# The first two weight chunks after a layer norm, taken one after the other instead of interleaved by K-tile

## The chip, the cores and the metric

The kernel runs on one core of a Trainium2 chip. The metric is device time in microseconds (us) for one execution of the whole program; lower is better. A core has a tensor engine (PE, with its weight loads shown as PEld), a vector engine (DVE), a scalar engine (ACT), a general engine (POOL) and a queue that starts DMAs (SP). Each runs its own instructions in order, and they meet through semaphores.

## The reference

512 tokens of 1024 features pass through a first block of two layers and then a second block of two layers. The part in which the change lies is the first block:

```python
for i in range(2):
    h = swiglu(x, ffn1_w_gate[i], ffn1_w_up[i], ffn1_w_down[i])
    x = layer_norm(ALPHA * x + 0.5 * h, ln_gain[i, 0], ln_bias[i, 0])
    m = pool_mixer(x, ...) if i == 0 else dilated_attention(x, ...)
    x = layer_norm(ALPHA * x + m, ln_gain[i, 1], ln_bias[i, 1])
    h = swiglu(x, ffn2_w_gate[i], ffn2_w_up[i], ffn2_w_down[i])
    x = layer_norm(ALPHA * x + 0.5 * h, ln_gain[i, 2], ln_bias[i, 2])
```

`swiglu(x, g, u, d)` is `(silu(x @ g) * (x @ u)) @ d` with 2816 hidden features. Everything is float32. After the first block come two layers with retention, sparse attention and gated linear attention, which the kernel calls `mixer`.

## The kernel before

Activations lie feature by feature: `x`, and its high and low parts `xh` and `xl`, are 8 K-tiles of 128 features by 512 tokens. A float32 product is made of three faster ones, `wh*xh + wh*xl + wl*xh`. POOL makes `wh` and `wl` out of the raw weights (L349, L353), chunk by chunk. A chunk is 1024 rows (8 K-tiles) by 256 columns, so two output tiles `m` of 128 features. It is split in four quarters of two K-tiles each. There are two slots for split weights, taken in turn: POOL may start on chunk c+2 only when PE has finished chunk c (it waits for `acc` at L342), and PE waits for each quarter (`wait_chunk`, L366). SP loads the raw weights ahead. One chunk for all 512 tokens is 2 x 8 x 3 = 48 matmuls of 512 columns.

The program is a list of stages: ffn 0, pool, ffn 1, ffn 2, attn, ffn 3, mixer, mixer. Between two of them lies a layer norm. It works in two halves of the tokens, h = 0 and h = 1, of 256 each. For each half DVE and ACT produce the normalized K-tiles in order: DVE scales tile m (L792), ACT writes `xh` (L719), DVE writes `xl` (L799) and raises `acts`. The tile is then ready for PE. DVE does all 8 tiles of half 0 and then all 8 of half 1. In between, after tile 5 of half 0 is scaled, DVE waits for the statistics of half 1 (L779). They come from PE: `pe_half_sums(before, 1)` (L521) issues matmuls against a matrix of ones at L534, ACT squares the result (L698) before it goes on with tile 5, and DVE goes on from there.

PE meets the new activations in `pe_first` (L546). It treats the first two chunks of the new stage, c and c+1, half by half, 6 matmuls of 256 columns for one K-tile of one chunk (L572):

- half 0: chunk c goes K-tile by K-tile as the tiles come, and chunk c+1 follows two K-tiles behind (`LAG = 2`). Ahead of the first two K-tiles stand 5 matmuls each that compute nothing (`pe_spin`, L544). After the third step stand the sums for half 1.
- half 1: chunk c first, K-tile by K-tile with a wait for each, and then chunk c+1 without any wait for activations.

Chunk c is finished, and its slot free for POOL, after chunk c of half 1. `pe_first` runs at five layer norms: before pool (border 0 in this text), ffn 1 (border 1), ffn 2 (border 2), attn (border 3, where a half is written in another order of tokens) and ffn 3 (border 4). The first ffn starts with `pe_begin`, and the borders into and between the mixers have `pe_entry` with an interleave of its own. After `pe_first` come whole chunks through `product` (L378, matmuls at L387) or `piece` (L889, matmuls at L1895), all with 512 columns.

Of the kernel before, what the change touches and what calls it, by code (L numbers as in the profile page):

```python
# [25 lines left out]
P = 128  # L26
# [3 lines left out]
KT = D // P  # L30
# [188 lines left out]
class Kernel:  # L219
# [326 lines left out]
    def pe_first(self, pe, st, residue=False):  # L546

        s, c = self.s, st.chunk0
        before = self.stages[self.stages.index(st) - 1]
        if before.kind == "start":  # L550
            self.pe_begin(pe, st)
            return
        for h in range(2):
            for step in range(2 * KT):
                for n in range(2):
                    k = step - (self.LAG, KT)[h] * n
                    if not 0 <= k < KT:
                        continue
                    if n == 0:
                        if h == 0 and k < 2:  # L560
                            self.pe_spin(self.VAR_BANK[1], 0, 5)
                        pe.wait_ge(s["acts"].sem, st.at("acts", KT * h + k + 1 - 2 * KT))
                    if (h, n, k) == (0, 1, 0):
                        pe.wait_ge(s["z_ready"].sem, st.at("z_ready", 0))
                    if h == 0 and k % 2 == 0:
                        self.wait_chunk(pe, c + n, k // 2)
                    xh, xl = (self.half(a[:, k], h, residue) for a in (self.xh, self.xl))
                    for m in range(2):
                        out = self.half(self.ps[:, 2 * n + m], h, residue)
                        w = slice(k * 256 + m * P, k * 256 + m * P + P)  # L570
                        for q, (a, b) in enumerate(((self.wh, xh), (self.wh, xl), (self.wl, xh))):
                            mm = self.nc.tensor.matmul(out, a[:, (c + n) % 2, w], b, start=k == 0 and q == 0, stop=k == KT - 1 and q == 2)  # L572
                        if h == 1 and k == KT - 1:
                            s["acc"].up(mm)
                if h == 0 and step == 2:
                    self.pe_half_sums(pe, before, 1)

    def pe_last(self, pe, st, chunks, xs, residue=False, sums=None):

        s = self.s  # L580
        xh, xl = xs
        at = 0
        sums = sums or self.pe_half_sums
        for n, (c, k, ready) in enumerate(chunks):
            last = n == len(chunks) - 1
            self.wait_chunk(pe, c)
            if ready:
                ready()
            for m, h in (((0, 0), (1, 0), (0, 1), (1, 1)) if last else ((0, 0), (0, 1), (1, 0), (1, 1))):
                if n == 0 and (m, h) == (0, 0) and "z_ready" in st.per:  # L590
                    pe.wait_ge(s["z_ready"].sem, st.at("z_ready", 4))
                out = self.tail_out(h, m, residue)
                for t in range(k):
                    if last and t == 3 and m != h:
                        sums(pe, st, 0, (2,) if h else (0, 1))
                    w = slice(t * 256 + m * P, t * 256 + m * P + P)
                    for q, (a, b) in enumerate(((self.wh, xh), (self.wh, xl), (self.wl, xh))):
                        mm = self.nc.tensor.matmul(out, a[:, c % 2, w], self.half(b(at + t), h, residue),  # L598
                                                   start=n == 0 and t == 0 and q == 0, stop=last and t == k - 1 and q == 2)
                if last and h == 0:  # L600
                    s["tail_mm"].up(mm)
                if h == 1:
                    s["acc"].up(mm)
            at += k
# [2404 lines left out]
```

## Time and profile before

| | us |
|---|---|
| median of 3 runs | 3483.22 |
| lowest and highest | 3482.59, 3483.66 |
| the profiled execution | 3485.5 |
| its span, first to last instruction | 3483.7 |

The profile is of one execution. Its page gives the busy time of each engine, the chain of work that ended last, and the costliest groups of instructions. The trace behind it gives every instruction with its start from the beginning of the span, its duration, and, where the engine stood idle ahead of it, what released it. Matmuls overlap each other, so their pace is read from the distance of their starts and not from their durations. The granted clock says which share of the full speed TensorE had: 1.00 is 2.4 GHz and 0.50 is 1.2 GHz.

### The profile page before, as it was taken

To read this page: it belongs to the slowest core of one execution; us is meant where nothing else is said; L and a number is where in the kernel's file an instruction comes from. 1 tells how busy PE (TensorE), PEld (TensorE's weight loads), DVE (VectorE), ACT (ScalarE), POOL (GpSimd) and SP (SyncE) were. 2 spreads that over 40 slices of the span, in tenths; PEclk is the share of its full clock that TensorE was granted. 3 is DMA by queue.
4 is the path that set the end of the run, shared out by engine and by line. 5 is a ranking of instruction groups with operands and counts; after the bars stand their busy time and mean duration, and the time that the engine had idled before them with its cause. 6 is when DMAs were issued, how large, how long until landed. Compare 5 with 4: busy or idle time off the path is not lost.

```text
span 3483.7 us, 48672 instructions
## 1 busy us (share of the span) xinstructions
PE 3421.0 (98%) x18708; PEld 2830.2 (81%) x18708; DVE 1503.3 (43%) x2307; ACT 822.7 (24%) x1463; POOL 2521.6 (72%) x2220
## 2 busy tenths in 40 slices
PE   9999989999999999999999999999999999999998
PEld 7887978888988888888888887877778787777876
DVE  5562562112311143344456114265656436565643
ACT  1110232110211022222234111122323222232322
POOL 9998787888788877665655888856566785655675
PEclk9999999999999999999999999999999999999999
DMA  6553222322233222122211332222222222222222
GB/s 220 189 182 102 83 85 85 96 93 92 93 96 95 89 93 88 63 72 73 73 62 49 108 96 94 85 82 67 62 72 67 85 85 85 64 61 76 64 82 73
DMA packets 322475, 312.08 MB, mean 90 GB/s; under 512 B 11616, under 2 KB 306176, under 8 KB 322048
## 3 DMA queue, kind: packets, MB, share of 16 engines
q1 hardware_dynamic: 304928, 277.91, 25.5%
q10 hardware_dynamic: 17376, 31.78, 2.8%
q8 instruction: 120, 1.97, 0.2%
q14 instruction: 51, 0.42, 0.0%
HBM read 307.56 MB, written 2.10 MB: 89 GB/s over the span
## 4 chain that ended last, share of the span: by engine, by line
PE 49%; issue 26%; POOL 21%; DVE 3%; ACT 1%; POOLq 0%; DMA 0%; DVEq 0%; SPq 0%
PE ps L1895 23%; POOL wh L349 14%; POOL wl L353 7%; PE ps L387 6%; PE ps L1566 4%; PE ps L598 3%; PE ps L1938 2%; PE ps L572 1%; PE ps L2471 1%; PE ps L1429 1%; PE ps L1475 1%; PE ps L2272 1%; PE ps L2243 1%; PE ps L905 1%; PE ps L1441 1%
## 5 line engine op out<-in xcount | busy, mean ns | idle before, releaser
L349 POOL TENSOR_TENSOR wh<-w_raw,zero 128x512 fp32r<-128x512 f32 (+3 forms) x1108 | 1156.0, 1054 | 931.4 <-PE ps L1895 379.1
L353 POOL TENSOR_TENSOR wl<-w_raw,wh 128x512 fp32r<-128x512 f32 (+3 forms) x1108 | 1423.0, 1295 | 0.0
L387 PE MATMUL ps<-xh,wh 128*128 128x512 f32 x1536 | 601.2, 391 | 2.7 <-POOL wl L353 1.5
L387 PE MATMUL ps<-xh,wl 128*128 128x512 f32 x1536 | 597.9, 389 | 0.0
L387 PE MATMUL ps<-xl,wh 128*128 128x512 f32 x1536 | 597.7, 389 | 0.0
L1895 PE MATMUL ps<-xh,wh 128*128 128x512 f32 x1072 | 444.0, 414 | 7.8 <-POOL wl L353 4.3
L1895 PE MATMUL ps<-xh,wl 128*128 128x512 f32 x1072 | 420.3, 392 | 0.0
L1895 PE MATMUL ps<-xl,wh 128*128 128x512 f32 x1072 | 420.2, 392 | 0.0
L387 PEld LDWEIGHTS ps<-xh,wh 128*128 128x128 f32 x1536 | 288.4, 188 | 65.5 <-POOL wl L353 3.4
L387 PEld LDWEIGHTS ps<-xl,wh 128*128 128x128 f32 x1536 | 288.4, 188 | 60.1 <-issue 1.0
L387 PEld LDWEIGHTS ps<-xh,wl 128*128 128x128 f32 x1536 | 288.3, 188 | 60.2
L1163 DVE TENSOR_TENSOR ps<-sg,ps 128x512 f32<-128x512 f32 x88 | 61.2, 695 | 583.9 <-PE ps L387 561.9
L1895 PEld LDWEIGHTS ps<-xh,wh 128*128 128x128 f32 x1072 | 202.0, 188 | 79.9 <-issue 22.6
L1895 PEld LDWEIGHTS ps<-xh,wl 128*128 128x128 f32 x1072 | 202.0, 188 | 44.9
L1895 PEld LDWEIGHTS ps<-xl,wh 128*128 128x128 f32 x1072 | 202.5, 189 | 41.1 <-issue 3.4
L387 PE MATMUL ps<-hid_h,wh 128*128 128x512 f32 x528 | 211.6, 401 | 3.8 <-POOL wl L353 2.1
L387 PE MATMUL ps<-hid_l,wh 128*128 128x512 f32 x528 | 209.5, 397 | 0.0
L387 PE MATMUL ps<-hid_h,wl 128*128 128x512 f32 x528 | 209.5, 397 | 0.0
L1144 ACT ACTIVATE hid_h<-ps 128x512 f32 x88 | 52.7, 598 | 447.4 <-DVE ps L1163 447.4
L387 PEld LDWEIGHTS ps<-hid_h,wh 128*128 128x128 f32 x528 | 99.6, 189 | 30.4 <-POOL wl L353 4.0
L387 PEld LDWEIGHTS ps<-hid_l,wh 128*128 128x128 f32 x528 | 99.5, 188 | 24.6 <-issue 1.0
L387 PEld LDWEIGHTS ps<-hid_h,wl 128*128 128x128 f32 x528 | 99.6, 189 | 24.0
(372 smaller groups left out, 6046.9 us busy)
## 6 DMA issues: line engine op xcount, KB each, us to landing
w_raw<-in_w_in SPq DMA_DIRECT2D x120, 512.0 KB, 4.1
w_raw<-in_ffn_w_gate SPq DMA_DIRECT2D x88, 512.0 KB, 4.7
w_raw<-in_ffn_w_up SPq DMA_DIRECT2D x88, 512.0 KB, 4.8
w_raw<-in_attn_w_qkv SPq DMA_DIRECT2D x72, 512.0 KB, 4.5
w_raw<-in_ffn_w_down SPq DMA_DIRECT2D x64, 512.0 KB, 3.6
ada_raw<-in_ada_w ACTq DMA_DIRECT2D x24, 512.0 KB, 3.9
stats<-in_ada_w ACTq DMA_DIRECT2D x24, 512.0 KB, 4.1
w_raw<-in_ffn_w_down SPq DMA_DIRECT2D x32, 384.0 KB, 4.0
```

The costliest lines, as they stand in the source:

```text
L349: done.append(s["w_hi"].up(pool.tensor_tensor(hi[:, parts[q]], raw[:, parts[q]], zero, ALU.subtract)))
L353: s["w_lo"].up(pool.tensor_tensor(lo[:, parts[q]], raw[:, parts[q]], hi[:, parts[q]].bitcast(F32), ALU.subtract))
L387: mm = self.nc.tensor.matmul(out, a[:, slot, w], b(t), start=start and t == order[0] and q == 0, stop=stop and t == order[-1] and q == 2)
L572: mm = self.nc.tensor.matmul(out, a[:, (c + n) % 2, w], b, start=k == 0 and q == 0, stop=k == KT - 1 and q == 2)
L598: mm = self.nc.tensor.matmul(out, a[:, c % 2, w], self.half(b(at + t), h, residue), start=n == 0 and t == 0 and q == 0, stop=last and t == ...
L905: mm = self.nc.tensor.matmul(out, a[:, (c + n) % 2, w], b, start=k == 0 and q == 0, stop=k == KT - 1 and q == 2)
L1144: s["hid_hi"].up(nc.scalar.activation(self.hid_h[:, 2 * i + m], self.ps[:, 2 + m], ACT.Copy))
L1163: t = s["hid"].up(nc.vector.tensor_tensor(product, self.sg[:, m], product, ALU.mult))
L1429: mm = nc.tensor.matmul(out, q[:, own], k, start=n == 0, stop=n == last)
L1566: mm = self.nc.tensor.matmul(out, x[t][:, r], b[:, c % 2, w], start=t == 0 and q == 0, stop=t == KT - 1 and q == 2)
L1895: mm = self.nc.tensor.matmul(out, a[:, slot, w], b(t), start=first and t == ks[0] and q == 0, stop=last and t == ks[-1] and q == 2)
L1938: mm = self.nc.tensor.matmul(out, x[t][:, r], b[:, c % 2, w], start=t == 0 and q == 0, stop=t == KT - 1 and q == 2)
```

## The change

Only `pe_first` is changed. Chunk c is taken alone, K-tile by K-tile, for half 0 and then for half 1, with the same waits and the same idle matmuls ahead of the first two K-tiles. The sums for half 1 stand after the fourth K-tile of half 0, no longer after the third step of the interleave. Only after all of chunk c comes chunk c+1, whole, with 512 columns, as 48 matmuls through `product`, first for m = 0 and then for m = 1. The wait for `z_ready` (that DVE has read what lies in the banks of chunk c+1) moves from the first matmul of chunk c+1 in half 0 to the head of this product.

```diff
         for h in range(2):
-            for step in range(2 * KT):
-                for n in range(2):
-                    k = step - (self.LAG, KT)[h] * n
-                    if not 0 <= k < KT:
-                        continue
-                    if n == 0:
-                        if h == 0 and k < 2:
-                            self.pe_spin(self.VAR_BANK[1], 0, 5)
-                        pe.wait_ge(s["acts"].sem, st.at("acts", KT * h + k + 1 - 2 * KT))
-                    if (h, n, k) == (0, 1, 0):
-                        pe.wait_ge(s["z_ready"].sem, st.at("z_ready", 0))
-                    if h == 0 and k % 2 == 0:
-                        self.wait_chunk(pe, c + n, k // 2)
-                    xh, xl = (self.half(a[:, k], h, residue) for a in (self.xh, self.xl))
-                    for m in range(2):
-                        out = self.half(self.ps[:, 2 * n + m], h, residue)
-                        w = slice(k * 256 + m * P, k * 256 + m * P + P)
-                        for q, (a, b) in enumerate(((self.wh, xh), (self.wh, xl), (self.wl, xh))):
-                            mm = self.nc.tensor.matmul(out, a[:, (c + n) % 2, w], b, start=k == 0 and q == 0, stop=k == KT - 1 and q == 2)
-                        if h == 1 and k == KT - 1:
-                            s["acc"].up(mm)
-                if h == 0 and step == 2:
+            for k in range(KT):
+                if h == 0 and k < 2:
+                    self.pe_spin(self.VAR_BANK[1], 0, 5)
+                pe.wait_ge(s["acts"].sem, st.at("acts", KT * h + k + 1 - 2 * KT))
+                if h == 0 and k % 2 == 0:
+                    self.wait_chunk(pe, c, k // 2)
+                xs = tuple((lambda t, a=a: self.half(a[:, t], h, residue)) for a in (self.xh, self.xl))
+                for m in range(2):
+                    mm = self.piece(c % 2, 256, m * P, self.half(self.ps[:, m], h, residue), xs, (k,), k == 0, k == KT - 1)
+                    if h == 1 and k == KT - 1:
+                        s["acc"].up(mm)
+                if (h, k) == (0, 3):
                     self.pe_half_sums(pe, before, 1)
+        pe.wait_ge(s["z_ready"].sem, st.at("z_ready", 0))
+        for m in range(2):
+            self.product(pe, (c + 1) % 2, KT, 256, m * P, self.ps[:, 2 + m], self.x_parts(),
+                         before=self.arrival(pe, c + 1, KT) if m == 0 else None)
```

## Rows read from the trace of the kernel before

**Rows 1.** The page: busy time, share and count of each engine; chain by engine.

```profile
PE 3421.0 (98%) x18708; PEld 2830.2 (81%) x18708; DVE 1503.3 (43%) x2307; ACT 822.7 (24%) x1463; POOL 2521.6 (72%) x2220
...
PE 49%; issue 26%; POOL 21%; DVE 3%; ACT 1%; POOLq 0%; DMA 0%; DVEq 0%; SPq 0%
```

**Rows 2.** Timeline of PE at border 2: start, duration, instruction, count, [idle before, releaser].

```profile
893.89 0.39 PE L572 MATMUL ps<-xh,wh 128*128 128x256 f32 x1 [0.34 <-DVE xl L799]
...
894.70 1.27 PE L544 MATMUL ps<-ones 128*128 128x128 f32 x10
...
899.01 0.38 PE L534 MATMUL ps<-stats,ones 128*128 128x256 f32 x1
```

**Rows 3.** Timeline of DVE at border 2.

```profile
897.73 1.12 DVE L799 SCALAR_TENSOR_TENSOR xl<-x,ln,xh 128x256 fp32r<-128x256 f32 x1
...
901.87 0.42 DVE L779 TENSOR_TENSOR stats<-ps,stats 128x256 f32<-128x256 f32 x1 [1.84 <-PE ps L534]
...
905.67 0.49 DVE L799 SCALAR_TENSOR_TENSOR xl<-x,ln,xh 128x256 fp32r<-128x256 f32 x1 [0.48 <-ACT xh L719]
...
908.45 0.48 DVE L799 SCALAR_TENSOR_TENSOR xl<-x,ln,xh 128x256 fp32r<-128x256 f32 x1 [0.19 <-ACT xh L719]
...
913.85 0.48 DVE L799 SCALAR_TENSOR_TENSOR xl<-x,ln,xh 128x256 fp32r<-128x256 f32 x1 [0.18 <-ACT xh L719]
```

**Rows 4.** Timeline of PE: last matmul of L572 at border 2, first of the next.

```profile
921.62 0.28 PE L572 MATMUL ps<-xh,wl 128*128 128x256 f32 x1
921.74 0.40 PE L387 MATMUL ps<-xh,wh 128*128 128x512 f32 x1
```

**Rows 5.** Timeline of PE: first matmul after L572 at borders 0, 1, 3, 4.

```profile
424.14 0.40 PE L387 MATMUL ps<-xh,wh 128*128 128x512 f32 x1
...
546.88 0.40 PE L387 MATMUL ps<-xh,wh 128*128 128x512 f32 x1
...
1298.92 0.40 PE L1895 MATMUL ps<-xh,wh 128*128 128x512 f32 x1
...
1911.34 0.40 PE L387 MATMUL ps<-xh,wh 128*128 128x512 f32 x1
```

**Rows 6.** Timeline of PE: the 49th matmul after border 1.

```profile
557.79 0.39 PE L387 MATMUL ps<-xh,wh 128*128 128x512 f32 x1
```

**Rows 7.** Timeline of DVE: last `xl` tile of half 1 at borders 0, 1, 3, 4.

```profile
416.24 0.48 DVE L799 SCALAR_TENSOR_TENSOR xl<-x,ln,xh 128x256 fp32r<-128x256 f32 x1 [0.18 <-ACT xh L719]
...
538.99 0.49 DVE L799 SCALAR_TENSOR_TENSOR xl<-x,ln,xh 128x256 fp32r<-128x256 f32 x1 [0.18 <-ACT xh L719]
...
1291.61 0.68 DVE L799 SCALAR_TENSOR_TENSOR xl<-x,ln,xh 128x256 fp32r<-128x256 f32 x1 [0.24 <-ACT xh L719]
...
1903.48 0.48 DVE L799 SCALAR_TENSOR_TENSOR xl<-x,ln,xh 128x256 fp32r<-128x256 f32 x1 [0.18 <-ACT xh L719]
```

**Rows 8.** Timeline of DVE: fourth `xl` tile of half 0 at borders 1 and 4.

```profile
522.18 1.12 DVE L799 SCALAR_TENSOR_TENSOR xl<-x,ln,xh 128x256 fp32r<-128x256 f32 x1
...
1887.33 0.87 DVE L799 SCALAR_TENSOR_TENSOR xl<-x,ln,xh 128x256 fp32r<-128x256 f32 x1
```

**Rows 9.** Timeline of PE: start of the sums for half 1 at borders 1 and 4.

```profile
524.15 0.59 PE L534 MATMUL ps<-stats,ones 128*128 128x256 f32 x2
...
1888.61 0.59 PE L534 MATMUL ps<-stats,ones 128*128 128x256 f32 x2
```

**Rows 10.** Timeline of POOL at border 2: the splitting of chunk c+2 begins.

```profile
916.23 2.04 POOL L349 TENSOR_TENSOR wh<-w_raw,zero 128x512 fp32r<-128x512 f32 x2 [13.84 <-PE ps L572]
```

**Rows 11.** Waits of PE, 424 to 464 us: us in total, times, longest.

```profile
PE ps L387 <- DVE y_l L1331: 7.7, 1, 7.7
PE ps L387 <- POOL wl L353: 1.0, 2, 0.6
```

**Rows 12.** Windows: stretch, us, then busy us (count) by engine, granted clock, DMA.

```profile
1869.00:1873.00 4.00, 1.90 (x11) 1.37 (x10) 2.63 (x3) 0.42 (x1) 4.00 (x4) 1.00 0.16 56
1873.00:1877.00 4.00, 4.00 (x22) 3.91 (x21) 0.29 (x1) 0.00 (x0) 2.81 (x3) 0.57 0.02 4
```

## The prediction

> **What bounds the kernel now.** I read the page first. PE is busy for 98% of the span and POOL for 72% [rows 1], so time is lost or won where PE gets work later, or gets more of it. The chain gives 21% to POOL [rows 1], which warns that weights may be late somewhere. Then I went to the five borders at which `pe_first` runs, one engine at a time. The first thing to see there is that PE has little idle time at all: at border 2 it waits 0.34 us ahead of the first K-tile [rows 2], and from the sums of half 1 on it runs without a gap into the next chunk at 921.74 [rows 4]. It has work for two chunks on every K-tile that DVE delivers, so DVE is not its limit. The second thing is when DVE ends: its last `xl` tile is done at 913.85 + 0.48 = 914.33 [rows 3], that is 7.4 us before PE leaves the border. The third is that POOL has stood idle 13.84 us until PE released chunk c's slot, and starts on chunk c+2 at 916.23 [rows 10], 5.5 us before PE wants its first quarter. So at a border PE bounds, and what it bounds with is stored work: half 1 of chunk c+1, which needs nothing that isn't there.
>
> **Part 1, the order.** The change keeps no work of chunk c+1 beside DVE's production. All of it goes behind DVE's last tile. PE then leaves the border at a time that can be summed: end of the last `xl` tile, plus what PE needs to take it up, plus the last K-tile of chunk c, plus the whole of chunk c+1, plus any delay of DVE itself.
> - Taking up a tile and doing it: the previous `xl` tile at border 2 ended 0.05 us before the matmul at 893.89, and the 6 matmuls of a K-tile that was waited for last from 893.89 to 894.70, 0.81 us [rows 2]. Together 0.86 us. DVE delivers the tiles of half 1 every (913.85 - 908.45) / 7 = 0.77 us [rows 3], and a K-tile not waited for costs PE 6 x 0.12 = 0.72 us (0.12 from the starts 921.62 and 921.74 [rows 4]), so PE keeps up and is at most a tenth behind at the end.
> - Chunk c+1 whole: 48 matmuls of 512 columns. After border 1 the first starts at 546.88 [rows 5] and the 49th at 557.79 [rows 6], so 10.9 us. Now the chunk costs 96 matmuls of 256 columns, 96 x 0.12 = 11.5 us. The change saves 0.6 us of PE work per border and moves 10.9 us to where nothing covers it.
>
> **Part 2, the sums of half 1.** DVE waits for them: at border 2 it stands idle 1.84 us until they are there, at 901.87 [rows 3]. ACT waits for them too before it goes on with tile 5, so all that both do afterwards shifts with them. Before, they start at 899.01 [rows 2]. In the new order they stand behind K-tile 3 of chunk c, whose `xl` ends at 897.73 + 1.12 = 898.85 [rows 3]. They can start at 898.85 + 0.86 = 899.71, 0.7 us later. Borders 0 and 3 have the same pattern; I take 0.7 there too. At border 4 the tile ends at 1888.20 [rows 8], the sums start at 1889.06 where they did at 1888.61 [rows 9]: 0.45. At border 1 the tile ends at 523.30 [rows 8], so 524.16 against 524.15 [rows 9]: nothing. No DMA is moved. The wait for `z_ready` comes later than before, when it has long been met; cost 0, and it covers nothing.
>
> **The sum by border**, as last `xl` end + delay + 0.86 + 10.9, less the start of the next chunk now:
> - border 0: 416.72 + 0.7 + 0.86 + 10.9 = 429.2, less 424.14 [rows 5, 7]: 5.0
> - border 1: 539.48 + 0 + 11.76 = 551.2, less 546.88: 4.4 [rows 5, 7]
> - border 2: 914.33 + 0.7 + 11.76 = 926.8, less 921.74: 5.1 [rows 3, 4]
> - border 3: 1292.29 + 0.7 + 11.76 = 1304.8, less 1298.92: 5.8 [rows 5, 7]
> - border 4: 1903.96 + 0.45 + 11.76 = 1916.2, less 1911.34: 4.8 [rows 5, 7]
>
> Together 25.1 us. **What of it is given back.** POOL gets chunk c's slot no later: PE finishes it at 914.33 + 0.7 + 0.86 = 915.9 at border 2, and POOL starts at 916.23 now [rows 10], so the same to within 0.2 us. It therefore has 4 to 5 us more ahead of PE's next chunk. That helps only where PE waits for it now: at border 0, 1.0 us in two waits [rows 11], which go. The lag isn't lost in the pooling stage's other wait, 7.7 us for DVE's `y_l` [rows 11]: DVE's work for the last group begins when PE has finished the fourth chunk, so it is late by as much. Behind the other borders the next chunk runs without a wait already. Leaves 24.1 us.
>
> **Part 3, the clock.** Between K-tile 7 of half 0 (its `xl` ends at 906.16) and K-tile 0 of half 1 (`xl` ends at 908.93 [rows 3]), PE, which is busy in that time now, will have about 2.8 - 0.8 = 2.0 us with nothing to do, and shorter idle times on both sides. The trace has such a place: from 1869 to 1873 us PE is busy 1.90 of 4.00 us, and in the next 4 us the granted clock is 0.57, the level of 1.2 GHz for most of it [rows 12]. That can happen at each border. Its price: a K-tile takes up to 0.72 us more while the clock is low. With 0.57 granted over 4 us, 4 x 0.43 = 1.7 us of full-speed work is missing. The lower bound is 0, where the low stretch falls on idle time; the upper 1.7 per border, 8.6 in all. I take 0.5 per border, 2.5 in all, since only part of the low stretch falls on the dense tiles of half 1. Less than 0 is excluded: no border has a low clock to give back but border 4, where it has recovered before the first K-tile.
>
> **A rule weighed.** Two matmuls of 256 columns take 0.24 us of PE's time, one of 512 takes 10.91 / 48 = 0.227 [rows 4 to 6]: merging gains 5%. The Trainium skill, "TensorE: Matmul & The Clock Gate", section "Back-to-back issue gap", gives 262 cycles for 256 columns and 518 for 512 at full clock, which is 0.109 and 0.216 us: a gain of 1%, so a change made for wider matmuls would win 0.1 us per border and not the 0.6 that the rows give, and chunk c+1 would take 10.4 us. By the page's figure the sum would be 5 x 0.5 = 2.7 us lower, an estimate. The rows are slower than the page for both widths, and I go by them.
>
> **Result.** 24.1 + 2.5 = 26.6 us. The profiled execution took 3485.5 us with a span of 3483.7; the median is 2.3 below it. Nothing in the difference depends on that, so 3483.2 + 26.6 = 3509.8 us, 0.76% slower.
>
> **Rivals.**
> - Not slower (the other side): PE's lag at the border is absorbed since POOL is the true limit behind it. POOL's start on chunk c+2 hangs on the release of chunk c alone, which doesn't move, and if PE waits for POOL in the next chunks anyway, the 24 us vanish and 5 x 0.6 = 3 us of narrow matmuls are won: 3480 us. It decides where the weights' waits behind a border exceed 4.4 us. For it: POOL's 21% of the chain [rows 1]. Against it: PE's only waits for POOL behind border 0 are 1.0 us [rows 11], and PE is busy 98%. Chance 0.04.
> - Less: one or two borders' lag is absorbed later, in waits of stages that hang on POOL or DVE and not on PE, or chunk c+1 goes faster than 10.9 us. 24.1 less two borders, 10: 3497 us. For it: PE is idle 62 us over the whole span [rows 1]. Against: most of these waits are chains that begin with a PE result. Chance 0.08.
> - More: the clock falls at every border and stays low over the dense tiles: 24.1 + 8.6, 3516 us. For it: the row above. Against: two borders have their idle time shorter or slower tiles, so that a slow PE keeps up. Chance 0.13.
> - The change does what it says; I see no way in which it doesn't, since order on PE is program order.
>
> **How the numbers follow.** Forecast 0.75, less 0.08, more 0.13, not slower 0.04. The range takes the clock from 0 to its bound and border 0's lag as partly absorbed: from 3500 (24.1 - 5 - 2.5) to 3516. Under 0.2% (7 us) can't be told from no change here. Slower by more than that: 0.95; within: 0.04; faster: 0.01.
>
> **What would show it.** Of the kernel after, at border 2: the first matmul of chunk c+2 some 33 us after the first K-tile's, where it is 27.9 now; PE waiting for DVE ahead of nearly every K-tile, with 5 to 7 us idle in sum; POOL starting on chunk c+2 as before, counted from the first K-tile; DVE's idle time ahead of L779 0.7 us longer at borders 0, 2, 3; no PE wait for POOL behind border 0; low granted clock in one window at most borders. I would be wrong if PE's idle time at the borders rose and the end didn't move, or if DVE's tiles came sooner when PE leaves them more room.

## The result and the profile after

The changed kernel takes 3511.96 us (median of 4 runs, 3509.70 to 3514.40) where the kernel before takes 3483.44 (median of 4, 3482.59 to 3485.43). The ratio is 1.0077, with a 95% interval from 1.0065 to 1.0089: slower by 28.5 us. The forecast was 3509.8, in a range from 3500 to 3516.

The span of the profiled execution grew from 3483.7 to 3509.7 us. From the page of the changed kernel, the same two lines as [rows 1]:

```profile
PE 3426.2 (98%) x18468; PEld 2823.2 (80%) x18468; DVE 1510.2 (43%) x2307; ACT 823.4 (23%) x1463; POOL 2523.3 (72%) x2220
...
PE 48%; issue 26%; POOL 20%; DVE 3%; ACT 1%; POOLq 0%; DMA 0%; DVEq 0%; SPq 0%
```

PE has 240 matmuls fewer, as it must (5 borders, 96 narrow for 48 wide), and is busy 5 us longer, while the span grew by 26. The page alone would not find that: the shares are the same to 1%. The borders show it. The timeline of PE at border 2 of the changed kernel (start, duration, instruction, count, [idle before, releaser]):

```profile
904.68 0.38 PE L1889 MATMUL ps<-xh,wh 128*128 128x256 f32 x1 [0.34 <-DVE xl L793]
...
909.70 0.39 PE L1889 MATMUL ps<-xh,wh 128*128 128x256 f32 x1 [0.44 <-DVE xl L793]
...
910.51 0.59 PE L534 MATMUL ps<-stats,ones 128*128 128x256 f32 x2
...
914.63 0.38 PE L1889 MATMUL ps<-xh,wh 128*128 128x256 f32 x1 [0.66 <-DVE xl L793]
...
916.08 0.39 PE L1889 MATMUL ps<-xh,wh 128*128 128x256 f32 x1 [0.48 <-DVE xl L793]
...
917.71 0.39 PE L1889 MATMUL ps<-xh,wh 128*128 128x256 f32 x1 [0.65 <-DVE xl L793]
...
920.49 0.39 PE L1889 MATMUL ps<-xh,wh 128*128 128x256 f32 x1 [1.80 <-DVE xl L793]
...
926.75 0.40 PE L387 MATMUL ps<-xh,wh 128*128 128x512 f32 x1
...
937.66 0.39 PE L387 MATMUL ps<-xh,wh 128*128 128x512 f32 x1
```

From the first K-tile to the first matmul of chunk c+2 it is now 937.66 - 904.68 = 32.98 us, where it was 921.74 - 893.89 = 27.85 [rows 2, 4]. PE waits for `xl` ahead of 8 of the 16 K-tiles, longest, 1.80 us, between the halves. Chunk c+1 starts at 926.75, after all tiles, and takes 10.91 us. The waits of PE in this border (total us, times, longest), first before from 893 to 922 us, then after from 904 to 938 us:

```profile
PE ps L572 <- DVE xl L799: 0.9, 3, 0.3
```

```profile
PE ps L1889 <- DVE xl L793: 4.9, 8, 1.8
```

DVE and POOL in the same border of the changed kernel, where [rows 3] and [rows 10] stood:

```profile
913.37 0.42 DVE L773 TENSOR_TENSOR stats<-ps,stats 128x256 f32<-128x256 f32 x1 [2.55 <-PE ps L534]
...
925.34 0.48 DVE L793 SCALAR_TENSOR_TENSOR xl<-x,ln,xh 128x256 fp32r<-128x256 f32 x1 [0.18 <-ACT xh L713]
```

```profile
927.00 2.04 POOL L349 TENSOR_TENSOR wh<-w_raw,zero 128x512 fp32r<-128x512 f32 x2 [13.81 <-PE ps L1889]
```

DVE waits 2.55 us for the sums (1.84 before) and ends its last tile at 925.82, that is 21.14 us after the first K-tile (20.44 before). POOL starts 22.32 us after it (22.34 before): its slot comes free at the same time.

The same reading of the traces at all five borders, in us. The forecast of the fourth column is without the clock's share. The fifth is the time from the last `xl` tile to the first matmul of chunk c+2:

| border | first K-tile to chunk c+2: before, after | difference | forecast | last `xl` to chunk c+2, after |
|---|---|---|---|---|
| 0 | 27.86, 32.97 | 5.1 | 5.0 | 11.82 |
| 1 | 26.80, 32.92 | 6.1 | 4.4 | 13.00 |
| 2 | 27.85, 32.98 | 5.1 | 5.1 | 11.84 |
| 3 | 30.01, 35.93 | 5.9 | 5.8 | 11.78 |
| 4 | 27.28, 33.21 | 5.9 | 4.8 | 12.91 |

The differences add up to 28.1 us; 26 of them are in the span. Border 1 has 1.7 us more than the forecast terms and border 4 has 1.1. In the fifth column these two stand 1.2 and 1.1 us above the others, and there the clock was low. The other 0.5 us of border 1 is DVE's: its last tile ends 19.93 us after the first K-tile where it ended at 19.39, although the sums start at the same time (4.08 us for 4.07). One `xl` tile, 7.66 us after the first K-tile in both kernels, took 0.48 us before and 1.59 after:

```profile
527.74 0.48 DVE L799 SCALAR_TENSOR_TENSOR xl<-x,ln,xh 128x256 fp32r<-128x256 f32 x1
```

```profile
532.45 1.59 DVE L793 SCALAR_TENSOR_TENSOR xl<-x,ln,xh 128x256 fp32r<-128x256 f32 x1
```

POOL was splitting weights at that moment in both kernels; why DVE took longer only in the second is not known. Windows of the changed kernel across border 1 (stretch, us, busy us and count of PE, PEld, DVE, ACT, POOL, granted clock, DMA share, GB/s):

```profile
536.50:540.50 4.00, 2.12 (x15) 1.88 (x15) 3.82 (x12) 1.42 (x3) 0.00 (x0) 0.99 0.49 170
540.50:544.50 4.00, 4.00 (x23) 4.00 (x22) 3.82 (x10) 2.54 (x5) 0.00 (x0) 0.58 0.02 4
```

After a stretch in which PE was busy 2.12 of 4 us, the clock is at its lower level, 1.2 GHz, for most of the next one, across the tiles of half 1. PE then falls behind DVE and ends 1.2 us later. A low clock does not always cost that. At border 3 it fell too:

```profile
1297.60:1301.60 4.00, 1.12 (x8) 0.77 (x6) 2.93 (x8) 1.56 (x3) 0.00 (x0) 1.00 0.09 28
1301.60:1305.00 3.40, 2.84 (x13) 2.84 (x14) 3.40 (x7) 2.48 (x4) 0.00 (x0) 0.50 0.00 0
```

The tiles of half 1 come more slowly there, every 0.98 us and not every 0.77, so PE has caught up before the last one, and the time from the last tile is the shortest of all, 11.78 us.

### The profile page after: what moved, and what is told of

Its sections match the earlier page's. It is cut to its first block, busy times and chain, and to the rows that moved or that the text cites. A ratio compares the mean times of both kernels' runs of the same rounds, so it can differ in the third digit from the quotient of the medians.

```text
span 3509.7 us, 48192 instructions
## 1 busy us (share of the span) xinstructions
PE 3426.2 (98%) x18468; PEld 2823.2 (80%) x18468; DVE 1510.2 (43%) x2307; ACT 823.4 (23%) x1463; POOL 2523.3 (72%) x2220
## 4 chain that ended last, share of the span: by engine, by line
PE 48%; issue 26%; POOL 20%; DVE 3%; ACT 1%; POOLq 0%; DMA 0%; DVEq 0%; SPq 0%
PE ps L1889 23%; POOL wh L349 14%; POOL wl L353 7%; PE ps L387 6%; PE ps L1560 4%; PE ps L592 3%; PE ps L1932 2%; PE ps L2465 1%; PE ps L1423 1%; PE ps L1469 1%; PE ps L2266 1%; PE ps L2237 1%; PE ps L899 1%; PE ps L1435 1%; PE ps L2251 0%
## 5 line engine op out<-in xcount | busy, mean ns | idle before, releaser
L387 PE MATMUL ps<-xh,wh 128*128 128x512 f32 x1616 | 632.1, 391 | 1.2 <-DVE xl L2789 1.2
L387 PE MATMUL ps<-xh,wl 128*128 128x512 f32 x1616 | 629.1, 389 | 0.0
L387 PE MATMUL ps<-xl,wh 128*128 128x512 f32 x1616 | 628.8, 389 | 0.0
L1889 PE MATMUL ps<-xh,wh 128*128 128x512 f32 (+1 forms) x1232 | 497.5, 404 | 32.3 <-DVE xl L793 24.6
L1889 PE MATMUL ps<-xl,wh 128*128 128x512 f32 (+1 forms) x1232 | 468.0, 380 | 0.0
L1889 PE MATMUL ps<-xh,wl 128*128 128x512 f32 (+1 forms) x1232 | 467.7, 380 | 0.0
L387 PEld LDWEIGHTS ps<-xh,wh 128*128 128x128 f32 x1616 | 303.4, 188 | 66.1 <-DVE xl L2789 2.0
L387 PEld LDWEIGHTS ps<-xh,wl 128*128 128x128 f32 x1616 | 303.3, 188 | 63.6
L387 PEld LDWEIGHTS ps<-xl,wh 128*128 128x128 f32 x1616 | 303.4, 188 | 63.1 <-issue 1.0
L1889 PEld LDWEIGHTS ps<-xh,wh 128*128 128x128 f32 x1232 | 234.8, 191 | 111.7 <-DVE xl L793 31.7
L1889 PEld LDWEIGHTS ps<-xh,wl 128*128 128x128 f32 x1232 | 234.8, 191 | 44.9
L1889 PEld LDWEIGHTS ps<-xl,wh 128*128 128x128 f32 x1232 | 235.1, 191 | 41.3 <-issue 3.4
L387 PEld LDWEIGHTS ps<-hid_h,wl 128*128 128x128 f32 x528 | 99.5, 188 | 24.1
```

Source lines behind the costliest of these rows:

```text
L387: mm = self.nc.tensor.matmul(out, a[:, slot, w], b(t), start=start and t == order[0] and q == 0, stop=stop and t == order[-1] and q == 2)
L1889: mm = self.nc.tensor.matmul(out, a[:, slot, w], b(t), start=first and t == ks[0] and q == 0, stop=last and t == ks[-1] and q == 2)
```

## The experiments

Times are medians; each is set against the kernel before on the same chip, where that had 3484.8 us for the first four kernels, 3485.7 for the next three and 3485.6 for the last three. The difference is what counts.

**The sums one K-tile earlier in the changed kernel.**

```diff
-                if (h, k) == (0, 3):
+                if (h, k) == (0, 2):
                     self.pe_half_sums(pe, before, 1)
```

> The changed kernel with the sums for half 1 put after K-tile 2 of half 0 in place of K-tile 3. Theory: behind a PE that has no stored work, the end of a border is the last xl tile plus 11.8 us, so whatever moves DVE moves the end one to one. The sums would start 4.4 us after the first K-tile at border 2 (5.83 in the changed kernel), so 1.4 us sooner at borders 0, 2 and 3, 0.7 at border 1 and 1.2 at border 4, together 6.2 us: about 3506 us. Rival: only the lost cover counts and the place of the sums costs nothing: 3512 us, with the end of border 2 still 33 us after its first K-tile.

3506.4 us, +21.5 over the kernel before; the changed kernel has +28.5, and +26.8 when it was run again (below). At border 2 (PE, DVE, PE):

```profile
902.72 0.39 PE L1889 MATMUL ps<-xh,wh 128*128 128x256 f32 x1 [0.34 <-DVE xl L793]
...
907.13 0.59 PE L534 MATMUL ps<-stats,ones 128*128 128x256 f32 x2
...
921.96 0.49 DVE L793 SCALAR_TENSOR_TENSOR xl<-x,ln,xh 128x256 fp32r<-128x256 f32 x1 [0.18 <-ACT xh L713]
...
935.30 0.39 PE L387 MATMUL ps<-xh,wh 128*128 128x512 f32 x1
```

The sums start 4.41 us after the first K-tile (5.83 in the changed kernel) and DVE ends at 19.73 (21.14): DVE follows the sums one to one. PE ends at 32.58 and not at 31.5, since the clock was low at this border, 12.9 us from the last tile. At border 1, where it was full, it is 11.82 and the border ends after 30.55 in place of 32.92; of these 2.4 us 1.2 are DVE's earlier end (18.73 for 19.93) and 1.2 the clock, which was low at border 1 in the changed kernel. Against the repeat, +26.8, the gain is 5.3 us and against the first comparison 7.0, around the 6.2 of the theory; the rival falls. A pair of kernels in which the clock cost nothing follows further below.

**The second chunk at its new place, but as two halves.** `product` is replaced by 2 x 8 x 2 calls of `piece` on 256 columns:

```diff
-        for m in range(2):
-            self.product(pe, (c + 1) % 2, KT, 256, m * P, self.ps[:, 2 + m], self.x_parts(),
-                         before=self.arrival(pe, c + 1, KT) if m == 0 else None)
+        for h in range(2):
+            for k in range(KT):
+                if h == 0 and k % 2 == 0:
+                    self.wait_chunk(pe, c + 1, k // 2)
+                xs = tuple((lambda t, a=a: self.half(a[:, t], h, residue)) for a in (self.xh, self.xl))
+                for m in range(2):
+                    mm = self.piece((c + 1) % 2, 256, m * P, self.half(self.ps[:, 2 + m], h, residue), xs, (k,), k == 0, k == KT - 1)
+                    if h == 1 and k == KT - 1:
+                        s["acc"].up(mm)
```

> The changed kernel, but chunk c+1 taken at its new place as two halves of 256 columns (96 matmuls) in place of 48 matmuls of 512. Theory: the wide product is what saves, 0.6 us at each of five borders, so this is 3 us slower than the changed kernel: about 3515 us, with 12.4 us from the last xl tile to the next chunk where 11.8 was measured. Rival: the wide product saves as little as the isolated figures say (0.1 us each) or costs something by its order (m = 0 whole, then m = 1): 3512 us or less.

3517.5 us, +32.6: some 4 to 6 us slower than the changed kernel. At border 2:

```profile
907.26 0.39 PE L1895 MATMUL ps<-xh,wh 128*128 128x256 f32 x1 [0.34 <-DVE xl L799]
...
940.84 0.40 PE L387 MATMUL ps<-xh,wh 128*128 128x512 f32 x1
```

33.58 us where the changed kernel has 32.98: the wide product saves 0.60 us, as the pace of 0.12 and 0.227 us said, and not 0.1. The rest of the difference, 1 to 3 us, fits the clock, which was low at four of the five borders here: border 0 alone, low for 6.8 us, has 14.69 us from the last tile where border 2 has 12.43.

**Half 0 of both chunks, then half 1 of both, not interleaved.** The loop over `n` comes back, but outside that over `k` (the head of the edit; the lines below it take chunk `c + n`, wait for tiles only where n is 0 and keep the sums after K-tile 3; the `product` at the end goes):

```diff
         for h in range(2):
-            for k in range(KT):
+            for n in range(2):
+                if (h, n) == (0, 1):
+                    pe.wait_ge(s["z_ready"].sem, st.at("z_ready", 0))
+                for k in range(KT):
```

> Half 0 of chunk c, then half 0 of chunk c+1 without waits, then half 1 of chunk c, then half 1 of chunk c+1, all with 256 columns and the sums after K-tile 3 as in the changed kernel. Theory: the loss is work of chunk c+1 that no longer lies beside DVE's tiles. Here half of it lies beside DVE's start of half 1; the next chunk starts 17.3 us after K-tile 7 of half 0 is done: +3.2 us against the kernel before at borders 0 and 2, +2.6, +2.2 and +3.0 at borders 1, 3 and 4, together 14 us: about 3498 us. Rival: what costs is only that the K-tiles of the two chunks aren't interleaved, so that PE waits ahead of each one of half 0; then this order gains nothing on the changed kernel: 3512 us.

3501.9 us, +17.1. From the first K-tile to chunk c+2 it is 3.3 us more than before at borders 0 and 2 and 3.0 at border 4 (3.2, 3.2 and 3.0 expected). At borders 1 and 3 it is 4.5 and 4.6 (2.6 and 2.2 expected), and there the clock was low. These two borders are 4.3 us over what was expected, more than the 3 us by which the time misses the forecast. That it is the clock fits the size at border 1, where 3.4 us at half speed leave 1.7 us of work undone and 1.9 are to be explained, but no run with a filled gap tested it in this order. Border 1:

```profile
529.00:533.00 4.00, 1.80 (x12) 1.57 (x12) 4.00 (x9) 3.15 (x6) 1.38 (x2) 0.98 0.29 74
533.00:537.00 4.00, 4.00 (x22) 3.77 (x21) 3.82 (x11) 1.42 (x3) 0.00 (x0) 0.59 0.54 188
```

Against the kernel before, 3.3 us are left of the 5.1 at borders 0 and 2, of which 0.7 is the later place of the sums. PE here waits 3.1 us for `xl` at border 2, against 4.9 in the changed kernel and 0.9 before. The order of the K-tiles as such is not what costs; the time that PE waits while it could do chunk c+1 is.

**The gap between the halves filled with idle matmuls.**

```diff
         for h in range(2):
+            if h == 1:
+                pe.wait_ge(s["z_ready"].sem, st.at("z_ready", 0))
+                self.pe_spin(3, 0, 7)
             for k in range(KT):
```

> The changed kernel with 7 idle matmul calls (1.75 us of PE, results thrown away) in the gap between half 0 and half 1 of chunk c, in a bank that nothing uses then. Theory: the low clock at some borders (3.4 us at borders 1 and 4 in the profile, with 13.0 and 12.9 us from the last xl tile to the next chunk in place of 11.8) comes from that gap. Then no border shows a low clock, all five show 11.8 us, and the median falls by 2 to 3 us to about 3509.5 with a narrower spread between runs. Rival: the low clock comes from the sparse K-tiles too or from nothing in this gap: 3512 us, and some border still shows it.

The 7 calls stand as 14 matmuls in the trace, 1.73 us. 3510.5 us, +25.7, and 11.83, 11.83, 11.83, 11.78 and 11.82 us from the last `xl` to chunk c+2 at the five borders: none slowed by the clock. Whether the time falls by as much needed the changed kernel beside it:

> The changed kernel once more, for its place beside the next one on the same chip and for which borders have the low clock in another execution. Theory: +27 to +29 us over the kernel before; 11.8 us from the last xl tile to the next chunk where the clock is full and 12.9 us where it is low, and not always at the same borders. Rival: the low clock belongs to borders 1 and 4 by their shape, so it stands there again and nowhere else.

> The changed kernel with the 7 idle calls between the halves once more, beside the changed kernel. Theory: 2 to 3 us faster than it, since no border has the low clock. Rival: no difference.

The changed kernel again: 3512.4 us, +26.8. With the filling again: 3511.3 us, +25.7. That is 1.1 us and not 2 to 3. The borders did as expected: 12.9, 13.0, 11.8, 11.8 and 12.9 us from the last tile in the changed kernel (borders 1 and 4 low as before, border 0 in addition, so the rival is half right; border 3 low too in either execution, and without a price), and 11.8 at all five with the filling. Three borders together gain 3.3 us. But 1.6 us of it is lost again at the end of attention, and some tenths in the stages between. The kernel before has 3.4 us of low clock at the end of attention [rows 12]. The changed kernel, shifted by 21.8 us, has none in that place, and the filled one has it again. Windows of the changed kernel in its first profile, at the work of [rows 12]:

```profile
1890.80:1894.80 4.00, 1.91 (x10) 1.36 (x8) 2.45 (x3) 0.42 (x1) 4.00 (x4) 1.00 0.12 38
1894.80:1898.80 4.00, 4.00 (x32) 3.86 (x31) 0.67 (x2) 0.80 (x2) 2.66 (x3) 1.00 0.01 4
```

PE is busy 1.90 of 4 us there in one kernel and 1.91 in the other; in one execution the clock falls and in the other not. So the low stretches are partly a matter of where an idle time happens to lie, and a gain at one place is paid back at another.

**The sums one step later in the kernel before.**

```diff
-                if h == 0 and step == 2:
+                if h == 0 and step == 3:
                     self.pe_half_sums(pe, before, 1)
```

> The kernel before with only the sums moved: after the fourth step of the interleave in place of the third, 1.4 us later. Theory: with the interleave PE has stored work and is itself the bound, so DVE's delay of 1.4 us per border reaches the end only as far as it uses up the 0.8 us between 7.4 us (last xl tile to the next chunk) and the least that can be, 6.6 us: 0.5 to 0.7 us per border, about 3 us in all, 3488 us where the kernel before has 3484.8. Rival: a delay of the sums always counts one to one, as it does in the changed kernel: 7 us, 3492 us.

3488.2 us, +2.5 (ratio 1.0007, interval 0.9998 to 1.0016). That interval holds 1, so the time alone doesn't show a loss; 7 us of the rival it does exclude, and the trace shows the rest. At border 2:

```profile
896.21 0.39 PE L572 MATMUL ps<-xh,wh 128*128 128x256 f32 x1 [0.34 <-DVE xl L799]
...
917.61 0.49 DVE L799 SCALAR_TENSOR_TENSOR xl<-x,ln,xh 128x256 fp32r<-128x256 f32 x1 [0.18 <-ACT xh L719]
...
924.78 0.40 PE L387 MATMUL ps<-xh,wh 128*128 128x512 f32 x1
```

DVE ends 1.45 us later against the first K-tile (21.89 for 20.44), and the border lasts only 0.7 us longer (28.57 for 27.85): the time from the last tile to the next chunk shrank from 7.4 us to the least it can be, 6.7. Borders 0, 1 and 4 lengthen by 0.7 us too. Border 3 lengthens by 1.5, all of DVE's delay: it stood at 6.63 us already in the kernel before, so no stored work was left there to hide it. With the interleave a delay of DVE is hidden by half where such work is left; without the interleave none of it is hidden, as the last pair below shows.

**The sums ahead of K-tile 1, in place of the second group of idle matmuls: in the kernel before and in the changed one.** In the kernel before:

```diff
-                        if h == 0 and k < 2:
+                        if h == 0 and k == 0:
                             self.pe_spin(self.VAR_BANK[1], 0, 5)
+                        if h == 0 and k == 1:
+                            self.pe_half_sums(pe, before, 1)
...
-                if h == 0 and step == 2:
-                    self.pe_half_sums(pe, before, 1)
```

> The kernel before with the sums for half 1 put ahead of K-tile 1 of half 0, where the second group of idle matmuls stood, which is taken out. Theory: PE bounds the border of the kernel before, so 1.25 us less PE work and up to 0.8 us less waiting make every border shorter by 1.3 to 2.0 us, and DVE, which waits 1.8 to 2.5 us for the sums, gets them in time (no idle time ahead of the variance): 8 us faster, about 3477 us against 3484.8. Rival: DVE or the taking up of K-tile 1, which now stands behind 2.5 us of sums, sets the end: no change.

> The changed kernel with the sums ahead of K-tile 1 in the same way. Theory: here DVE's last tile sets the end, and DVE gets rid of its whole wait for the sums, 2.5 us at each of five borders: 12.5 us less than the changed kernel, about 3501 us, with 11.8 us from the last xl tile to the next chunk as before. Rival: PE's own work is what counts, and only the 1.25 us of idle matmuls per border come back: 3507 us.

On the kernel before: 3476.4 us, 9.2 us less than the kernel before (ratio 0.9973, interval 0.9961 to 0.9984). It beats both kernels. At border 2 (PE, DVE, PE):

```profile
890.59 0.39 PE L574 MATMUL ps<-xh,wh 128*128 128x256 f32 x1 [0.34 <-DVE xl L799]
...
891.41 0.59 PE L534 MATMUL ps<-stats,ones 128*128 128x256 f32 x2
...
896.66 0.41 DVE L779 TENSOR_TENSOR stats<-ps,stats 128x256 f32<-128x256 f32 x1
...
916.31 0.40 PE L387 MATMUL ps<-xh,wh 128*128 128x512 f32 x1
```

The variance has no idle time ahead of it any more, and the border takes 25.72 us where it took 27.85. The five borders gain 2.1, 1.1, 2.1, 1.4 and 1.6 us, over 8 together. How much of it comes from the earlier sums and how much from the idle matmuls that went, 1.25 us of PE at each border, was not separated.

On the changed kernel: 3503.7 us, +18.1, where +16 was expected. DVE ends 2.2 us sooner at border 2 (18.96 for 21.15 after the first K-tile; 2.1 to 2.2 at every border and not the 2.5 of the theory), and the time from the last tile is 12.4 to 13.0 us at all five borders, so the low clock takes 0.6 to 1.2 us of it each time. That was tested too, with the gap filled as above:

> The changed kernel with the sums ahead of K-tile 1 and also 7 idle matmul calls (1.75 us) in the gap between the halves. Theory: the low clock stood at all five borders of the kernel with the early sums alone, 12.4 to 13.0 us from the last xl tile to the next chunk; filled, the gap shows 11.8 us everywhere and the time falls by 4 to 5 us against the same kernel without the filling (+18 us over the kernel before on its chip), so to +13 to +14 us. Rival: the clock falls because of the waits ahead of single K-tiles, which the filling doesn't touch: +18 us.

3498.2 us, +12.6: 5.4 us less, and 11.8 us at every border. Windows across border 2, first with the early sums alone, then with the gap filled as well:

```profile
911.00:915.00 4.00, 2.07 (x12) 1.86 (x13) 3.81 (x12) 1.42 (x3) 0.00 (x0) 0.90 0.69 238
915.00:919.00 4.00, 4.00 (x26) 4.00 (x26) 3.82 (x11) 2.54 (x5) 0.00 (x0) 0.67 0.00 0
```

```profile
914.00:918.00 4.00, 3.76 (x32) 3.56 (x31) 3.81 (x12) 1.75 (x4) 0.00 (x0) 1.00 0.60 210
918.00:922.00 4.00, 4.00 (x33) 3.91 (x32) 3.66 (x10) 2.22 (x5) 0.00 (x0) 1.00 0.00 0
```

So filling the gap between the halves takes away what the low clock cost at the borders, 0.6 to 1.2 us for each where it had a price. It does not keep the clock up everywhere: border 3 had a low stretch of 3.4 us in two of the three executions with the gap filled, again without a price. That the gap is the whole cause is therefore not shown.

Two of the kernels with the gap filled also give the price of a delay of DVE in the new order without the clock. Border 2 with the gap filled, first with the sums after K-tile 3, then with the early sums:

```profile
902.43 0.38 PE L1892 MATMUL ps<-xh,wh 128*128 128x256 f32 x1 [0.34 <-DVE xl L796]
...
923.09 0.48 DVE L796 SCALAR_TENSOR_TENSOR xl<-x,ln,xh 128x256 fp32r<-128x256 f32 x1 [0.18 <-ACT xh L716]
...
935.41 0.39 PE L387 MATMUL ps<-xh,wh 128*128 128x512 f32 x1
```

```profile
902.90 0.39 PE L1892 MATMUL ps<-xh,wh 128*128 128x256 f32 x1 [0.34 <-DVE xl L796]
...
921.36 0.48 DVE L796 SCALAR_TENSOR_TENSOR xl<-x,ln,xh 128x256 fp32r<-128x256 f32 x1 [0.19 <-ACT xh L716]
...
933.66 0.39 PE L387 MATMUL ps<-xh,wh 128*128 128x512 f32 x1
```

DVE ends 2.20 us sooner (18.94 for 21.14) and the border is 2.22 us shorter (30.76 for 32.98): one to one.

Even so the changed order with both remedies stays 22 us behind the order before with one of them (+12.6 against -9.2).

## Why the prediction was right

**Part 1, the order.** It named the end of a border as the last `xl` tile plus 0.86 plus 10.9 us. Where the clock cost nothing it is 11.82, 11.84 and 11.78 us (borders 0, 2, 3) for 11.76. The product of chunk c+1 takes 10.91 us. The experiment with part of the cover given back came out at three of its borders to 0.1 us as worked out.

**Part 2, the sums.** 0.7 us of delay were summed for border 2; the sums start 0.71 us later against the first K-tile (5.83 for 5.12), DVE waits 2.55 for 1.84, and its last tile moves by 0.70. At borders 3 and 4 DVE's end moved by 0.77 and 0.40 for 0.7 and 0.45. At border 1 the term was 0 and DVE ended 0.54 us later, not because of the sums. That the delay counts in full behind the new order, and by half behind the old one at four of five borders, was shown by moving the sums in either kernel.

**What is given back.** This term was off in two parts, which nearly cancel. At border 0 PE is 4.85 us late when it enters chunk c+2, and when it leaves chunk c+3 it is 3.14 us late, 450.75 for 447.61:

```profile
447.61 0.40 PE L387 MATMUL ps<-y_h,wh 128*128 128x512 f32 x1
...
463.87 0.76 PE L387 MATMUL ps<-y_h,wh 128*128 128x512 f32 x1 [7.70 <-DVE y_l L1331]
```

```profile
450.75 0.40 PE L387 MATMUL ps<-y_h,wh 128*128 128x512 f32 x1
...
467.95 0.77 PE L387 MATMUL ps<-y_h,wh 128*128 128x512 f32 x1 [8.63 <-DVE y_l L1325]
```

So the two waits for POOL, which did go, gave back 1.7 us and not the 1.0 us of [rows 11]: the view counts idle time from a matmul's end, but the starts around the two waits lie 0.74 and 0.84 us further apart than at the usual pace. The longer wait behind it did not move with PE. It grew from 7.7 to 8.6 us, and PE comes out of it 4.08 us late. The prediction had DVE's last group begin when PE has finished the fourth chunk; in the changed kernel DVE comes to it straight from the group before, without idle time, 3.6 us later than before (453.74 for 450.13), and takes 0.5 us longer for it. A longer low clock in this stage (10.2 us for 6.8) adds 0.6, and PE enters border 1 4.7 us late. Of 4.85 us 0.15 were given back where 1.0 was forecast.

**Part 3, the clock.** 2.5 us in all was the least certain term. In the profile the borders lost 1.2 and 1.1 us, border 0's stage 0.6, and the end of attention won 1.6: 1.3 net. The bound of 1.7 us per border held in the changed kernel; with narrow halves border 0 lost 2.3. "Less than 0 is excluded" looked only at the borders: what the change shifted at the end of attention was a gain. The longest idle time between the halves was 1.80 us at border 2 for the 2.0 worked out.

**The sum.** By the profiles it is 25.1 for the order and the sums at the borders, and 0.3 more in small parts; 0.5 for DVE at border 1; 1.3 for the clock; less 0.8 given back by the two waits behind border 0 (1.7 won, 0.9 lost again); less 0.4 elsewhere: 26.0 us, the growth of the span. The forecast had 24.1 and 2.5, 26.6. The large term was right by its mechanism; that the small ones came to the same total is luck. The medians differ by 28.5 in one comparison and 26.8 in the other; the executions of the changed kernel spread over 4.7 us in the first. The lower end of the range, 3500, also took 2.5 us of clock off 24.1, in which no clock was contained; without that it would have been 3502, and the measured time lies inside either way.

**The signs.** The first matmul of chunk c+2 comes 32.98 us after the first K-tile for 33, POOL starts as before, DVE's idle time ahead of L779 (now L773) is 0.7 to 0.8 us longer at borders 0, 2 and 3, and no wait for POOL is left in the two chunks behind border 0. PE waited for DVE less than was said: ahead of half of the K-tiles, not nearly every one, and 4.9 us at border 2, not 5 to 7. The clock was low at three of five borders.

**The rule weighed.** The Trainium skill, "TensorE: Matmul & The Clock Gate", section "Back-to-back issue gap", gives for the gap of an isolated matmul 262 cycles at 256 columns and 518 at 512. By that, 0.109 and 0.216 us, the wide product would save 0.1 us per border, an estimate; the experiment with narrow halves measured 0.6. The measured pace is slower at both widths, 0.120 and 0.227 us, so the rows were the right base.

**The rivals.** "Not slower" would have needed waits for POOL behind the borders. POOL was released at the same time, and the lag of borders 1 and 2 stays in full until the next border (10.83 us after border 1, 10.79 at the first K-tile of border 2), that of border 4 to the end of the span. "Less" didn't come about, and "more" only in part: at border 3 the clock fell too, and a slow PE kept up with the slower tiles, as was said against it.

## What to carry to other kernels

Where one engine follows a producer tile by tile, look for what it can do that has no need of the newest tile, and keep that beside the production. The end of such a stretch is the producer's last tile plus what is left to do then, and merging that into wider instructions won 0.6 us where the lost cover cost 5. Then ask what the producer itself waits for: here a few matmuls placed 4 us earlier at each of five borders, in place of idle ones, were worth 9 us. A delay of the producer counts only by what it exceeds the stored work (1.45 us of it cost 0.7 where 0.7 was stored, and 1.5 where none was), so the same edit has another price in either order.

## What the hardware showed

The price of a low clock at a border was not steady, and neither was its occurrence. One low stretch of 3.4 us cost 0.8 to 1.2 us at borders 0, 1, 2 and 4 of the changed order and nothing at border 3, where the producer's tiles come more slowly; 6.8 us of it cost 0.2 and 0.6 us at border 3. In the profiles of five executions with the gap unfilled (the changed kernel twice, the sums one K-tile earlier, the narrow halves, the early sums) it cost time at two to five of the five borders; the same kernel had this at borders 1 and 4 in one execution and at 0, 1 and 4 in the other. In the three with the gap filled it cost none at any border, though the clock was low for 3.4 us at border 3 in two of them. What decides between two executions of the same kernel was not tested.

A matmul of 512 columns came every 0.227 us and two of 256 every 0.240, also where the same chunk was done in the one form and in the other at the same place.
